# RMSNorm of a two-layer decoder, tile by tile, inside the FFN's output projection

## What is computed

```python
def rmsnorm(x, w):
    y = x * rsqrt(mean(x * x, axis=-1) + EPS)
    return y * w

h = x                                        # 2048 tokens x 1024, float32, for each core
for layer in range(2):
    hn = rmsnorm(h, norm_mix_w[layer])
    # layer 0: gated short convolution and HGRN2 recurrence; layer 1: retention with rotary phase
    h = h + mixer(hn) @ w_out[layer]
    hn = rmsnorm(h, norm_ffn_w[layer])
    gate, up = split(hn @ ffn_w_in[layer])   # 2 x 2816 columns
    h = h + (silu(gate) * up) @ ffn_w_out[layer]
return rmsnorm(h, norm_final_w)
```

## Time and profile before

| | |
|---|---|
| median of the runs | 2334.04 us (2332.65 and 2335.43) |
| profiled execution | 2332.21 us |
| its span on the slowest core | 2330.7 us (cores: 2321.4 to 2330.7) |
| PE busy | 1972.7 us, 85% |
| DVE busy | 1144.1 us, 49% |
| ACT busy | 803.6 us, 34% |
| POOL busy | 511.5 us, 22% |
| chain that ended last | PE 73%, DVE 10%, ACT 6%, issue 5%, DMA 3% |
| mean granted PE clock | 0.921 of full speed |

### The profile page before, as it was taken

One profiled execution on the slowest core, in us unless ns is written; L12 is line 12 of the kernel. 1 busy time (PEld: TensorE's weight loads), 2 busy tenths in 40 slices (PEclk: granted clock), 3 DMA queues, 4 the chain that ended last, 5 costly groups with the idle time before them and its releaser, 6 DMA issues.

```text
span 2330.7 us, 34132 instructions; the slowest of 8 cores (2321.4 to 2330.7 us)
## 1 busy us (share of the span) xinstructions
PE 1972.7 (85%) x11304; PEld 1080.0 (46%) x11304; DVE 1144.1 (49%) x2158; ACT 803.6 (34%) x1333; POOL 511.5 (22%) x504
## 2 busy tenths in 40 slices
PE   1798669994899999995598998998994999999990
PEld 1343257772444444443265564563662444444440
DVE  1465546663424241436667575675773233232343
ACT  5114766665410101025055163262466211101003
POOL 0111223332000000000354654654651000000000
PEclk9999879996799999996799898998995899999995
DMA  4533100004031232141000502304103123222003
GB/s 151 73 38 47 19 10 1 2 2 55 7 46 30 37 46 37 29 54 41 14 11 1 78 2 32 46 2 60 19 2 55 19 37 46 37 41 41 10 1 153
DMA packets 105851, 83.23 MB, mean 36 GB/s; under 512 B 11664, under 2 KB 91792, under 8 KB 105552
## 3 DMA queue, kind: packets, MB, share of 16 engines
q0 software_dynamic: 98688, 60.83, 19.6%
q1 hardware_dynamic: 6992, 20.22, 2.6%
HBM read 133.46 MB, written 8.39 MB: 61 GB/s over the span
## 4 chain that ended last, share of the span: by engine, by line
PE 73%; DVE 10%; ACT 6%; issue 5%; DMA 3%; POOL 2%; DVEq 0%; SPq 0%; ACTq 0%; POOLq 0%
PE pm L356 71%; ACT junk L371 3%; PE pm L365 2%; DVE hnT L375 2%; ACT arena L369 2%; POOL arena L375 2%; DVE arena L385 1%; DVE arena L375 1%; ACT L369 1%; DVE h L375 1%; DVE arena L381 1%; DVE arena L379 1%; DMA h<-x 1%; DVE arena L545 1%; DMA out<-arena 1%
## 5 line engine op out<-in xcount | busy, mean ns | idle before, releaser
L356 PE MATMUL pm<-hnT,wring 128*128 128x512 bf16 x3968 | 883.5, 386 | 91.1 <-ACT arena L369 41.6
L369 ACT ACTIVATE arena<-pm 128x512 f32<-128x512 f32 (+4 forms) x528 | 305.8, 592 | 1090.4 <-PE pm L356 975.1
L356 PEld LDWEIGHTS pm<-hnT,wring 128*128 128x128 bf16 x3968 | 392.5, 99 | 581.4 <-issue 130.9
L375 DVE TENSOR_TENSOR arena<-pm,arena 128x256 f32<-128x256 f32 (+3 forms) x544 | 261.3, 514 | 619.0 <-PE pm L356 573.5
L356 PE MATMUL pm<-wring,arena 128*128 128x512 bf16 x2176 | 518.8, 390 | 47.4 <-DVE h L375 41.6
L375 POOL TENSOR_TENSOR arena<-arena 128x512 bf16<-128x512 f32 (+3 forms) x320 | 349.0, 1094 | 549.7 <-ACT arena L369 252.6
L375 DVE TENSOR_TENSOR h<-pm,h 128x512 f32<-128x512 f32 x448 | 308.6, 689 | 212.6 <-PE pm L356 206.8
L356 PE MATMUL pm<-wring,hnT 128*128 128x256 bf16 (+1 forms) x3072 | 360.0, 276 | 28.7 <-POOL arena L375 24.9
L356 PEld LDWEIGHTS pm<-wring,arena 128*128 128x128 bf16 x2176 | 204.4, 99 | 314.8 <-issue 98.2
L356 PEld LDWEIGHTS pm<-wring,hnT 128*128 128x128 bf16 (+1 forms) x3072 | 311.6, 103 | 69.4 <-issue 43.1
L369 ACT ACT_TABLE_LOAD x188 | 241.2, 1283 | 255.6 <-POOL arena L375 117.6
(11 more groups left out here) (41 smaller groups left out, 703.6 us busy)
## 6 DMA issues: line engine op xcount, KB each, us to landing
wring<-ffn_w_in POOLq DMA_DIRECT2D x44, 512.0 KB, 7.2
wring<-odd_w_in POOLq DMA_DIRECT2D x24, 512.0 KB, 10.2
wring<-ffn_w_out POOLq DMA_DIRECT2D x22, 512.0 KB, 8.7
h<-x SPq DMA_DIRECT2D x16, 512.0 KB, 12.2
out<-arena SPq DMA_DIRECT2D x16, 512.0 KB, 2.6
wring<-even_w_in POOLq DMA_DIRECT2D x10, 512.0 KB, 12.0
wring<-odd_w_out POOLq DMA_DIRECT2D x8, 512.0 KB, 16.2
wring<-even_w_out POOLq DMA_DIRECT2D x4, 512.0 KB, 14.9
```

The costliest lines, as they stand in the source:

```text
L356: S.op("pe", lambda e: e.matmul(out, lhsT=lhsT, rhs=rhs, start=start, stop=stop), reads, writes, inc)
L369: S.op("act", lambda e: e.activation(out=out, in_=in_, func=func, scale=scale), reads, writes)
L375: S.op(eng, lambda e: e.tensor_tensor(out=out, in0=in0, in1=in1, op=op), reads, writes)
```

## The change

The statistics are computed for each tile separately: `norm_rstd(t)` does the square, TENSOR_SCALAR, Sqrt and RECIPROCAL on one column of `nst`, and `norm_tile(t)` continues at once with the copy, the transposes and the product of that tile. The two norms ahead of the FFNs and the first one are loops of `norm_tile` over the tiles, at their old places. `out_proj_add` gets a callback, which the last group of an FFN uses: behind the matmuls and adds of tile t it issues the norm of tile t-1, and behind the last tile that of tile T-1. In FFN 0 the callback is the norm ahead of the second mixer, in FFN 1 the final norm with its output DMA. The final weight and the two output buffers are allocated, and the weight is loaded, at the start of FFN 1.

```diff
--- before.py
+++ after.py
@@ -418,39 +418,43 @@
     xn = [sbt("xn%d" % i, [128, D], BF16) for i in range(2)]
     r_xn = [Res(), Res()]
     nst = sbt("nst", [128, 64], F32)
-    r_nst = Res()
-
-    def norm_stats():
-        for t in range(T):
-            ACT(junk[:], h[:, t, :], AF.Square, [r_h[t]], [r_junk, r_nst], accum_out=nst[:, t:t + 1])
-        TS("dve", nst[:, 16:16 + T], nst[:, 0:T], 1.0 / D, EPS, ALU.mult, ALU.add, [r_nst], [r_nst])
-        ACT(nst[:, 16:16 + T], nst[:, 16:16 + T], AF.Sqrt, [r_nst], [r_nst])
-        RECIP(nst[:, 32:32 + T], nst[:, 16:16 + T], [r_nst], [r_nst])
-
-    def rmsnorm_to_hnT(wcol):
-        norm_stats()
+    r_nst = [Res() for _ in range(T)]
+
+    def norm_rstd(t):
+        rn = r_nst[t]
+        ACT(junk[:], h[:, t, :], AF.Square, [r_h[t]], [r_junk, rn], accum_out=nst[:, t:t + 1])
+        TS("dve", nst[:, 16 + t:17 + t], nst[:, t:t + 1], 1.0 / D, EPS, ALU.mult, ALU.add, [rn], [rn])
+        ACT(nst[:, 16 + t:17 + t], nst[:, 16 + t:17 + t], AF.Sqrt, [rn], [rn])
+        RECIP(nst[:, 32 + t:33 + t], nst[:, 16 + t:17 + t], [rn], [rn])
+
+    def norm_tile(t, wcol):
+        norm_rstd(t)
         wb = wcol.unsqueeze(2).to_broadcast([128, KD, 128])
-        for t in range(T):
-            x_, rx = xn[t % 2], r_xn[t % 2]
-            ACT(x_[:], h[:, t, :], AF.Copy, [r_h[t], r_nst], [rx], scale=nst[:, 32 + t:33 + t])
-            pt, rpt = tbank()
-            for k in range(KD):
-                TR(pt[:, k * 128:(k + 1) * 128], x_[:, k * 128:(k + 1) * 128], 128, [rx], [rpt], inc=(k == KD - 1))
-            TT("dve", hnT[:, :, t * 128:(t + 1) * 128], pt[:].rearrange("p (k c) -> p k c", k=KD), wb, ALU.mult,
-               [rpt, r_nw], [r_hn[t]])
+        x_, rx = xn[t % 2], r_xn[t % 2]
+        ACT(x_[:], h[:, t, :], AF.Copy, [r_h[t], r_nst[t]], [rx], scale=nst[:, 32 + t:33 + t])
+        pt, rpt = tbank()
+        for k in range(KD):
+            TR(pt[:, k * 128:(k + 1) * 128], x_[:, k * 128:(k + 1) * 128], 128, [rx], [rpt], inc=(k == KD - 1))
+        TT("dve", hnT[:, :, t * 128:(t + 1) * 128], pt[:].rearrange("p (k c) -> p k c", k=KD), wb, ALU.mult,
+           [rpt, r_nw], [r_hn[t]])
 
     def hn_reads(g):
         return r_hn[g * TPG:(g + 1) * TPG]
 
-    def out_proj_add(lhs_fn, nk, rhs_fn, reads):
+    def out_proj_add(lhs_fn, nk, rhs_fn, reads, after_tile=None):
         for t in range(T):
             for half in range(2):
                 p, rp = bank()
                 PROJ(p[:, :], [lhs_fn(j, t) for j in range(nk)], [rhs_fn(j, half) for j in range(nk)], reads(t), [rp])
                 hs = h[:, t, half * 512:(half + 1) * 512]
                 TT("dve", hs, p[:, :], hs, ALU.add, [rp, r_h[t]], [r_h[t]])
-
-    rmsnorm_to_hnT(nmw[:, 0, :])
+            if after_tile is not None and t >= 1:
+                after_tile(t - 1)
+        if after_tile is not None:
+            after_tile(T - 1)
+
+    for t in range(T):
+        norm_tile(t, nmw[:, 0, :])
     phase()
     mixT = BA.alloc(4 * SL).rearrange("p (c s) -> p c s", c=4)
     r_mix = [Res() for _ in range(NG)]
@@ -699,10 +703,12 @@
     for w_ in whi + whg + weo:
         W.done(w_[0])
     S.barrier()
-
-    def ffn(l):
-        rmsnorm_to_hnT(nfw[:, l, :])
+    for t in range(T):
+        norm_tile(t, nfw[:, 0, :])
+
+    def ffn(l, tail_setup, tail_tile):
         phase()
+        tail_setup()
         actT = [BA.alloc(6 * SL).rearrange("p (c s) -> p c s", c=6) for _ in range(2)]
         r_act = [[[Res() for _ in range(NG)] for _ in range(6)] for _ in range(2)]
         sgt = [FA.alloc(GS), FA.alloc(GS)]
@@ -733,13 +739,13 @@
             nk = 2 * len(grp)
             out_proj_add(lambda j, t: aT[:, j, t * 128:(t + 1) * 128], nk,
                          lambda j, half: wts[j // 2][1][:, j % 2, half * 512:(half + 1) * 512],
-                         lambda t: [rA[j][t // TPG] for j in range(nk)] + [w_[2] for w_ in wts])
+                         lambda t: [rA[j][t // TPG] for j in range(nk)] + [w_[2] for w_ in wts],
+                         after_tile=(tail_tile if gi == len(ffn_groups()) - 1 else None))
             for w_ in wts:
                 W.done(w_[0])
 
-    ffn(0)
-
-    rmsnorm_to_hnT(nmw[:, 1, :])
+    ffn(0, lambda: None, lambda t: norm_tile(t, nmw[:, 1, :]))
+
     phase()
     cosT = FA.alloc(SL)
     sinT = FA.alloc(SL)
@@ -924,21 +930,26 @@
         for w_ in wv + wg_ + wo_:
             W.done(w_[0])
         S.barrier()
-
-    ffn(1)
-
-    phase()
-    fw = FA.alloc(D)
-    r_fw = Res()
-    S.dma("sp", fw, dr["norm_final_w"].partition_broadcast(128), writes=[r_fw])
-    norm_stats()
-    ot = [FA.alloc(D), FA.alloc(D)]
-    r_ot = [Res(), Res()]
+    for t in range(T):
+        norm_tile(t, nfw[:, 1, :])
+
+    fin = {}
     ov = out_d.rearrange("(t p) d -> p t d", p=128)
-    for t in range(T):
-        o_, ro = ot[t % 2], r_ot[t % 2]
-        STT(o_, h[:, t, :], nst[:, 32 + t:33 + t], fw, ALU.mult, ALU.mult, [r_h[t], r_nst, r_fw], [ro])
+
+    def final_setup():
+        fin["fw"] = FA.alloc(D)
+        fin["r_fw"] = Res()
+        S.dma("sp", fin["fw"], dr["norm_final_w"].partition_broadcast(128), writes=[fin["r_fw"]])
+        fin["ot"] = [FA.alloc(D), FA.alloc(D)]
+        fin["r_ot"] = [Res(), Res()]
+
+    def final_tile(t):
+        norm_rstd(t)
+        o_, ro = fin["ot"][t % 2], fin["r_ot"][t % 2]
+        STT(o_, h[:, t, :], nst[:, 32 + t:33 + t], fin["fw"], ALU.mult, ALU.mult, [r_h[t], r_nst[t], fin["r_fw"]], [ro])
         S.dma("sp", ov[:, t, :], o_, reads=[ro])
+
+    ffn(1, final_setup, final_tile)
     assert W.consumed == len(W.lst)
     S.finish("sp")
     return nc
```

## The result

The changed kernel takes 2458.96 us (median), the kernel before 2335.14; the ratio is 1.0534, 95% interval 1.051 to 1.0558. It is 5.3% slower. The forecast was 2459 us. The profiled execution took 2455.77 us with a span of 2453.9, against 2332.21 and 2330.7.

A forecast was written before the change was run, and what follows sets the result against it. The prediction took the five RMSNorms, where PE waits, as where the kernel stands still. Terms +24.9, +29.7, +29.8, +59.3 and -18.7 sum to +125.0 on 2332.2, plus 1.8 for the median: 2459 us, range 2428 to 2485.

The forecast's parts named there:

- The chain: Separate norms: each tile's TENSOR_SCALAR waits for the previous product, sixteen rounds of 4.48 us; +24.9, +29.7 and +29.8 us.
- The FFN 0 tail: Norm inside FFN 0's last output projection: rounds of 7.1 us with PE's clock dropping after each pause; +59.3 us.
- The final norm: Inside FFN 1's last output projection, no transposes or copy: rounds of 3.8 us, output-buffer waits gone; -18.7 us.
- No extra table loads: ScalarE in the norms: Square and Copy run under the square-root table, so the new order adds no loads.
- rival B: Square needs another table than Sqrt in the new order: 77 loads of 1.28 us, +99, 2558 us; chance 0.03.
- estimate of 205 us: ScalarE: 77 more table switches at the skill's 2.66 us each; the prediction set it aside as nothing by the trace.
- Rival A: All norms: neighbouring tiles' chains overlap, each norm bound by its busiest engine; -29 in total, 2305 us; chance 0.04.

The follow-up runs named there:

- overlapped kernel: Changed kernel's same instructions reissued so each step handles parts of four tiles (final norm: three): 2282.93 us, ratio 0.978; run again, 2280.66 us, ratio 0.9763.

## Why the prediction was right

*The chain.* Shown. A round was costed at 4.48 us and is 4.52. The errors fell on either side: product and next TENSOR_SCALAR overlap by 0.08, and RECIPROCAL to product took 2.83 (656.64 to 659.47) where I had 2.68. That one edit of the order takes the three norms from 75 to 40 us shows it as the cause; that TENSOR_SCALAR(t+1) stood behind product(t) in every round is in the rows. The transposes ran at the low clock in these rounds (1.01 us for eight, against 0.61 in the tail at the full clock); as the links came from the earlier trace rows, the price had that in it.

*The FFN 0 tail.* A round of 7.1 was forecast, the mean is (1199.32 - 1099.65 - 1.3) / 14 = 7.03. The two bounds were 5.7 and 7.6: with the clock held up it is 5.5, the slowest rounds are 7.5 (1115.53 to 1122.99). The reading of the earlier trace rows, that a pause of some 3 us costs the clock and half of a burst, came out nearly as it stood, though not in each round: pauses of 3.04 us ended at either level. That it is PE's order that makes the pause, the prediction said; that the product's place hardly matters there it left open, and the kernel with the deferred product showed it (rounds of 6.87 us). With the clock held up it might matter: in the kernel with the added matmuls the adds start directly behind the product (1148.77 and 1149.91 of its trace), without a wait for PE. That wasn't tried.

*The final norm.* Right in its mechanism and 4.6 us too small. I had 3.8 us for a round and it is 3.47 (2431.67 to 2435.14 in the rows below): I added joins of 0.1 where queued VectorE instructions overlap, and 14 rounds of 0.33 are the 4.6.

```profile
2431.67 0.14 DVE L381 TENSOR_SCALAR nst<-nst 128x1 f32<-128x1 f32 x1
...
2432.54 1.28 DVE L385 SCALAR_TENSOR_TENSOR arena<-h,nst,arena 128x1024 f32<-128x1024 f32 x1 [0.17 <-DVE nst L392]
...
2435.14 0.14 DVE L381 TENSOR_SCALAR nst<-nst 128x1 f32<-128x1 f32 x1
```

The waits for the output buffers are gone, as said.

*No extra table loads.* The page of the profile has 188 of them before and after; rival B is out. The load in the first norm is 1.28 us, and the Sqrt starts 0.01 behind it (19.67 and 20.96 in the trace after), so a switch adds 1.3 us here. The Trainium skill, ScalarE: Activation LUTs, section "What ACT_TABLE_LOAD costs", has about 2.66 us for every switch to a different set; this row doesn't bear that out, and the prediction's estimate of 205 us by that figure didn't come, as no switch was added.

*Rival A.* Its mechanism didn't happen in this kernel, but it is what the overlapped order makes. Even so its price was too high: 2305 us, where 2281 to 2283 are measured, for the same reason as in the experiment (durations added up on an engine whose neighbours overlap).

The errors of the terms cancel in part (+0.8, +0.4, +0.8, -1.1, -4.6, and +2.3 outside), so that the total is nearer than its parts deserve; the forecast lies 3 us above the 2455.92. That it is even closer to the median of all executions is luck.

## What to carry over

To pipeline tiles it isn't enough to put them beside other work: with engines that run their lists in order, the next tile's first step must be issued ahead of this tile's last. Write down for each engine the list of one round, follow the hand-overs, and take the sum around the loop as the price of a tile; batched phases that look wasteful may be what hides the hand-overs. When a step is moved into another engine's stream, ask what is queued behind its wait: here PE's own matmuls, and then PE's clock.

## What the runs showed of the hardware

- Neighbours that don't depend on each other overlap a little on VectorE (0.08 us) and ScalarE (about 0.1 us); in the overlapped kernel a copy of 1.13 us, a square of 1.04 with its read of 0.18 and a root of 0.18 make 2.17 us a tile, not their sum of 2.5.
- A pause of 3.04 us in each round ended in part of the rounds at the full clock (transposes 0.61 us) and in part at the low one (1.01), with the same program and the same pauses.
- With a product every 3.47 us no product waited for its output buffer; in the overlapped kernel, at 2.7 us, none did either until the last two, which came without adds between them (1.03 and 0.36 us).
